# Scaling attention probabilities on GpSimd before they are turned, without a turned block of reciprocal sums, and three output products at the head of each cycle

## The chip, the cores and the metric

The kernel runs on one core of a Trainium2 chip. The metric is the device time of one execution in microseconds. The unchanged kernel took 2381.67 us, the median of three runs (2380.95 to 2384.39).

## The reference

The program is one inference step of a two-layer encoder trunk over a prompt of 2048 tokens and 8 samples of 16 tokens. Layer 0 mixes tokens by softmax attention in a band of chunks, layer 1 by a gated recurrence; each layer has a cross-attention into 256 memory tokens, a gate and an output projection. The change lies in the attention of layer 0 over the prompt:

```python
s = jnp.einsum('bcqhd,bckhd->bchqk', qc, kb).astype(F32) * (HD_A ** -0.5)
s = s + rel_bias_lookup(table, dist)
s = jnp.where(valid[None, :, None, None, :], s, NEG)
p = jax.nn.softmax(s, axis=-1).astype(v.dtype)
o = jnp.einsum('bchqk,bckhd->bcqhd', p, vb)
...
y = jnp.concatenate([mix_o, cross_attn(xq, mk, mv)], axis=-1) * jax.nn.silu(gate)
return x + y @ w
```

The softmax divides each query's exponentials by their sum. Everything is float32.

## The kernel before

The function `prompt_band` does the attention, the gating and the output projection of layer 0. A *tile* T is 128 tokens: T = 0 holds the samples, T = 1 to 16 the prompt. A tile has eight *pairs* p of heads, six of band attention (p < 6) and two of cross-attention (p = 6, 7). A *unit* is u = 8T + p. A band unit of tile T looks at n = min(T, 5) tiles of 128 keys, a cross unit at n = 2. Prompt units are worked two at a time; a *cycle* is the two units u and u+1, so a tile has four cycles, p = 0, 2, 4, 6, and the prompt has 64.

The order on each engine is written out by hand; engines meet only at semaphores. One unit and head h goes through these steps:

- TensorE `scores` (L2321, for cross units L2308) makes query by key products in PSUM.
- VectorE `low_min` adds the bias, negates and finds the row minimum (L2524, for cross units L2512).
- ScalarE `exp` (L2676) writes the exponentials into the SBUF tile `se` and their sum into `tot`.
- TensorE `turn` (L2352) turns `se` by 128x128 transposes into PSUM, n of them.
- ScalarE `low` (L2683) and VectorE `high` (L2541) copy the turned blocks to `pt` in SBUF.
- TensorE `values` (L2408) multiplies them with the values into the PSUM bank `OB`, which is transposed: its partitions are head columns, its columns are tokens.

The exponentials are not divided. Instead VectorE takes the reciprocals of both heads' sums in one instruction (`inverse`, L2530), GpSimd spreads them to a 128x128 block `rb` (`spread`, L2221), TensorE turns that block as one more transpose behind the second head's (L2356), VectorE copies it with the second head's high part, and GpSimd multiplies the gate by it (L2230). VectorE's `gate` (L2578) then multiplies `OB` by that gate for four units at once.

TensorE's order within a cycle is `turn(u,0)`, three products, `turn(u,1)`, three products, `turn(u+1,0)`, three products, `turn(u+1,1)`, three products, then `scores(u+2)`, `scores(u+3)`, `values(u)`, `values(u+1)`. The products (L2453) are those of the output projection of the tile before, 48 a tile. In the first cycle of tiles 2 to 16 the group that would stand between `turn(u+1,0)` and `turn(u+1,1)` stands ahead of `turn(u,0)` instead. VectorE's order is four copies with a reciprocal behind the first, one sum or low part (L2591 or L2583), four `low_min` of the next two units, a reciprocal, and after p = 2 and p = 6 the `gate`. GpSimd also issues the store of each finished tile (L2214), once a tile. In tile 1 VectorE also makes low parts of the weights (L2570).

Of the kernel before, what the change touches and what calls it, by code (L numbers as in the profile page):

```python
# [16 lines left out]
ALU = mybir.AluOpType  # L17
# [3 lines left out]
P = 128  # L21
# [1905 lines left out]
def prompt_band(nc, l, sem, sb_in, sb_far_in, ps_in, v, early, opening):  # L1927
# [8 lines left out]
    FIRST = (6, 0, 7, 1, 2, 3, 4, 5)  # L1936
    s_sc, s_min, s_exp, s_rs, s_tp, s_eva, s_evd, s_pv, s_gr = (
        sem(f"pb_{n}") for n in ("sc", "min", "exp", "rs", "tp", "eva", "evd", "pv", "gr"))
    s_tv, s_va, s_vd, s_y, s_yh, s_yl, s_op, s_xadd, s_bias, s_rb = (
        sem(f"pb_{n}") for n in ("tv", "va", "vd", "y", "yh", "yl", "op", "xadd", "bias", "rb"))  # L1940
    s_kt, s_kea, s_ked, s_tk, s_tka, s_tkd, s_off, s_wl, s_wh = (
        sem(f"pb_{n}") for n in ("kt", "kea", "ked", "tk", "tka", "tkd", "off", "wl", "wh"))
    s_ldk, s_ldx = ([sem(f"pb_{n}{i}") for i in range(2)] for n in ("ldk", "ldx"))
# [8 lines left out]
    with ExitStack() as ctx:  # L1952
# [71 lines left out]
        def tiles_of(T, p):  # L2024
            if T == 0:
                return 4 if p < XP else 3
            return min(T, RING) if p < MG else NMEM // P
# [17 lines left out]
        def gate_loads(job):  # L2045
            return 16 * (job // 2 + 1) + (16 if job % 2 == 0 else 0)
# [32 lines left out]
        with nc.Block() as block:  # L2079
# [130 lines left out]
            @block.gpsimd  # L2210
            def _(pool):
                def store(job):
                    pool.wait_ge(s_xadd, 2 * job + 2)
                    pool.dma_start(v["x_mid"][tile_of(job)], xt[job % 2][:]).then_inc(s_stx[job % 2], 16)  # L2214

                def spread(u):

                    at = 2 * (u % 2)
                    pool.wait_ge(s_rs, u + 1)
                    wait(pool, s_tp, 2 * u - 2)  # L2220
                    nc.gpsimd.tensor_copy(rb[u % 2][:].rearrange("p (h n) -> p h n", n=HD),  # L2221
                                          rs[:, at:at + 2].unsqueeze(2).to_broadcast([P, 2, HD])).then_inc(s_rb, 1)
                for u in range(U_ALL):
                    T, p = step(u)
                    n = tiles_of(T, p)
                    spread(u)
                    if p == 0:
                        pool.wait_ge(s_ldg[T % 2], gate_loads(T))
                    pool.wait_ge(s_evd, 2 * u + 2)
                    nc.gpsimd.tensor_tensor(gt[T % 2][:, p], gt[T % 2][:, p], pt[u % 2][1][:, n * P:(n + 1) * P], ALU.mult  # L2230
                                            ).then_inc(s_gr, 1)
                    if T == 0 and p == 5:
                        pool.wait_ge(s_pb1, 16)
                        pool.wait_ge(s_gr, u + 1)
                        nc.gpsimd.memset(bias[0:64, :, BAND - CHUNK:], BIG).then_inc(s_bias, 1)
                        pool.wait_ge(s_bias, 1)
                    if T == 1 and p == MG:
                        pool.wait_ge(s_pb2, 16)
                        pool.wait_ge(s_gr, u + 1)
                        nc.gpsimd.memset(bias[64:P, :, 0:CHUNK], BIG).then_inc(s_bias, 1)  # L2240
                        pool.wait_ge(s_bias, 2)
                    if T and p == PAIRS - 1:
                        store(T - 1)
                for t in range(early.COUNT):
                    early.root(nc, pool, t)

            @block.tensor
            def _(pe):
# [79 lines left out]
                def turn(u, h):  # L2328

                    T, p = step(u)  # L2330
                    n = tiles_of(T, p)
                    low = low_of(n)
                    done = 2 * u + h
                    to = turned_to(u, h)
                    pe.wait_ge(s_exp, done + 1)
                    if T == 0:
                        wait(pe, s_eva, done)
                        wait(pe, s_evd, done)
                    elif u % 2 == 0:
                        pe.wait_ge(s_exp if is_cross(T, p) else s_min, 2 * u + 3)  # L2340
                    elif h == 0 and u % 2:
                        pe.wait_ge(s_eva, 2 * u - 1)
                        pe.wait_ge(s_evd, 2 * u - 1)
                    if u == 0 and h == 0:
                        pe.wait_ge(s_tka, 1)
                        pe.wait_ge(s_tkd, 1)
                    if T == 0 and p == MG + 1 and h == 0:
                        pe.wait_ge(s_va, 2)
                        pe.wait_ge(s_vd, 2)
                    for i in range(n):  # L2350
                        at = i * P if i < low else 512 + (i - low) * P
                        ins = nc.tensor.transpose(to[:, at:at + P], se[u % 2][h][:, i * P:(i + 1) * P], ident[:])  # L2352
                    if h:
                        pe.wait_ge(s_rb, u + 1)
                        at = 512 + (n - low) * P
                        ins = nc.tensor.transpose(to[:, at:at + P], rb[u % 2][:], ident[:])  # L2356
                    ins.then_inc(s_tp, 1)
# [121 lines left out]
                scores(PAIRS + 1)  # L2479
                for u in range(PAIRS, U_ALL, 2):  # L2480
                    T, p = step(u)
                    lead = 3 if p == 0 and T > 1 else 0
                    project(T - 1, 6 * p, 6 * p + lead)
                    turn(u, 0)
                    project(T - 1, 6 * p + lead, 6 * p + 3 + lead)
                    turn(u, 1)
                    project(T - 1, 6 * p + 3 + lead, 6 * p + 6 + lead)
                    turn(u + 1, 0)
                    project(T - 1, 6 * p + 6 + lead, 6 * p + 9)
                    if p == MG and T < NT:  # L2490
                        turn_values(T + 1)
                    turn(u + 1, 1)
                    project(T - 1, 6 * p + 9, 6 * p + 12)
                    if u + 2 < U_ALL:
                        scores(u + 2)
                        scores(u + 3)
                    values(u)
                    values(u + 1)
# [6 lines left out]
            def _(dve):  # L2505
# [21 lines left out]
                def inverse(u):  # L2527
                    at = 2 * (u % 2)
                    dve.wait_ge(s_exp, 2 * u + 2)
                    nc.vector.reciprocal(rs[:, at:at + 2], tot[:, at:at + 2]).then_inc(s_rs, 1)  # L2530

                def high(u, h):
                    T, p = step(u)
                    n = tiles_of(T, p)
                    low = low_of(n)
                    dve.wait_ge(s_tp, 2 * u + h + 1)
                    if h:
                        wait(dve, s_gr, u - 1)
                    width = (n - low + h) * P
                    if width:  # L2540
                        ins = nc.vector.tensor_copy(pt[u % 2][h][:, low * P:low * P + width], turned_to(u, h)[:, 512:512 + width])  # L2541
                    else:
                        ins = nc.vector.memset(pt[u % 2][h][:, BAND:BAND + 1], 0.0)
                    ins.then_inc(s_evd, 1)
# [76 lines left out]
                        values_high(1)  # L2621
                low_min(PAIRS + 1, 0)
                low_min(PAIRS + 1, 1)
                inverse(PAIRS)
                for u in range(PAIRS, U_ALL, 2):
                    T, p = step(u)
                    high(u, 0)
                    inverse(u + 1)
                    high(u, 1)
                    if u == PAIRS:  # L2630
                        weights_low(5)
                    high(u + 1, 0)
                    if p == MG and T < NT:
                        values_high(T + 1)
                    if u == PAIRS:
                        weights_low(6)
                    high(u + 1, 1)
                    if p % 4 == 0:
                        low_part(T - 1 if p == 0 else T, 1 - p // 4)
                    else:  # L2640
                        add(T - 1, p // 4)
                    if u + 2 < U_ALL:
                        for v in (u + 2, u + 3):
                            low_min(v, 0)
                            low_min(v, 1)
                        inverse(u + 2)
                    if u == PAIRS:
                        weights_low(7)
                    if p % 4 == 2:
                        dve.wait_ge(s_pv, u + 2)  # L2650
                        dve.wait_ge(s_gr, u + 2)
                        gate(T, p // 4)
                low_part(NT, 1)
                for i in range(4):
# [12 lines left out]
            def _(act):  # L2667
                def exp(u, h):
                    T, p = step(u)
                    at = 2 * (u % 2) + h  # L2670
                    act.wait_ge(s_min, 2 * u + h + 1)
                    if u >= 2:
                        act.wait_ge(s_rs, u - 1)
                    n = tiles_of(T, p) * P
                    src = scores_at(u, h, u % 2, NMEM // P) if is_cross(T, p) else se[u % 2][h][:, 0:n]
# [24 lines left out]

                def keys_out_low(n, dst):
                    act.wait_ge(s_tk, n + 1)
                    if n:
                        act.wait_ge(s_gr, U_ALL)
                    nc.scalar.copy(dst[:, 0:384], TP[:, 0:384]).then_inc(s_tka, 1)

                def weights_high(i):
# [784 lines left out]
```

## Time and profile before

| | us |
|---|---|
| median of three runs | 2381.67 |
| span of the profiled execution | 2376.1 |
| busy: TensorE matmul, VectorE, ScalarE, GpSimd | 2312.2, 1819.5, 1413.5, 381.0 |
| prompt tiles of the stage that changes | about 700 to 1260 |

The profile is of one execution. It gives its span from the first to the last instruction and no other time of its own; the median of the runs is 5.6 us above that span. The table of busy times covers the whole program, so it tells little about this stage, which is about a quarter of it. Rows of the stage itself stand below.

### The profile page before, as it was taken

The page shows a single profiled execution, that of the slowest core. Times are in us where ns is not written, and L with a number is a line of the kernel's source. Part 1 is how long each engine was busy: PE and PEld are TensorE (multiplying, and loading weights), DVE is VectorE, ACT ScalarE, POOL GpSimd, SP SyncE. Part 2 cuts the span into 40 slices and gives each one's busy share as a digit, 9 for nine tenths or more (in the row PEclk, how much of TensorE's full clock was granted, in tenths as well). Part 3 has the DMA queues.
Part 4 walks back from the last instruction along what each step waited for, and adds up shares of the span by engine and source line. Part 5 has one row for each costly group of instructions (what it writes and reads, how often), then busy time and mean ns, then how long its engine had stood idle before and what let it go on. Part 6 is the DMA issues. An engine that isn't in the chain of part 4 may idle for free. (4 is left out here: it accounts for less than half of the span.)

```text
span 2376.1 us, 61711 instructions
## 1 busy us (share of the span) xinstructions
PE 2312.2 (97%) x23787; PEld 2094.7 (88%) x23787; DVE 1819.5 (77%) x3555; ACT 1413.5 (59%) x3281; POOL 381.0 (16%) x585
## 2 busy tenths in 40 slices
PE   7999999999989999999999999999999989999998
PEld 4999999999967888888887999999999978888886
DVE  7889788887666656666666998797888777888885
ACT  4564666755565555555554564776757566666664
POOL 2332000000022221211112332000000112112111
PEclk9999999999999999999999999999999999999999
DMA  6886887769894222222226897886879793444442
GB/s 227 298 299 219 301 281 231 247 220 332 232 307 121 83 66 89 90 69 83 73 81 232 272 303 242 256 275 214 266 248 312 230 269 117 129 131 122 137 135 70
DMA packets 396664, 469.64 MB, mean 198 GB/s; under 512 B 39860, under 2 KB 248556, under 8 KB 396376
## 3 DMA queue, kind: packets, MB, share of 16 engines
q1 hardware_dynamic: 379832, 406.02, 54.4%
q0 software_dynamic: 14704, 54.92, 6.6%
q10 hardware_dynamic: 1840, 4.75, 0.7%
q8 instruction: 193, 3.16, 0.5%
q14 instruction: 95, 0.78, 0.1%
HBM read 318.77 MB, written 151.56 MB: 198 GB/s over the span
## 5 line engine op out<-in xcount | busy, mean ns | idle before, releaser
L1468 PE MATMUL pj_acc<-x_lo,pj_wh 128*128 128x256 f32 (+1 forms) x3080 | 780.9, 284 | 0.0
L1468 PE MATMUL pj_acc<-x_hi,pj_wh 128*128 128x256 f32 (+1 forms) x3080 | 780.8, 284 | 0.0
L1468 PEld LDWEIGHTS pj_acc<-x_hi,pj_wh 128*128 128x128 f32 x3080 | 578.4, 188 | 0.0
L1468 PEld LDWEIGHTS pj_acc<-x_lo,pj_wh 128*128 128x128 f32 x3080 | 578.4, 188 | 0.0
L509 ACT ACTIVATE pj_wh<-pj_wt 128x512 fp32r<-128x512 f32 x676 | 420.3, 634 | 255.9 <-DMA pj_wt<-tsum 175.1
L516 DVE SCALAR_TENSOR_TENSOR pj_wl<-pj_wt,pj_wh 128x512 fp32r<-128x512 f32 x676 | 467.0, 708 | 87.0 <-ACT pj_wh L509 79.3
L1464 PE MATMUL pj_acc<-x_hi,pj_wl 128*128 128x256 f32 (+1 forms) x3080 | 509.4, 287 | 13.8 <-DVE pj_wl L516 11.9
L1464 PEld LDWEIGHTS pj_acc<-x_hi,pj_wl 128*128 128x128 f32 x3080 | 425.3, 188 | 22.1 <-DVE pj_wl L516 19.5
L1307 DVE TENSOR_TENSOR pj_out<-pj_out,pj_acc 128x512 f32<-128x512 f32 (+1 forms) x448 | 320.8, 716 | 103.3 <-PE pj_acc L1468 69.7
L2541 DVE COPY pb_pt<-pb_SCTP 128x256 f32<-128x256 f32 (+2 forms) x266 | 115.8, 435 | 147.5 <-PE pb_SCTP L2352 74.3
L2676 ACT ACTIVATE pb_se<-pb_se,pb_mn 128x640 f32<-128x640 f32 (+4 forms) x208 | 154.6, 745 | 114.6 <-DVE pb_mn L2524 114.3
L2683 ACT COPY pb_pt<-pb_SCTP 128x384 f32<-128x384 f32 (+2 forms) x272 | 106.3, 391 | 123.7 <-PE pb_SCTP L2356 62.9
L2524 DVE CUSTOM_DVE_ANT_0 pb_se<-pb_SCTP,pb_bias 128x640 f32<-128x640 f32 (+4 forms) x204 | 137.6, 727 | 44.0 <-PE pb_SCTP L2321 38.8
L2352 PE MATMUL pb_SCTP<-ident,pb_se 128*128 128x128 f32 x1020 | 156.9, 276 | 3.9 <-ACT pb_se L2676 2.6
L2352 PEld LDWEIGHTS pb_SCTP<-ident,pb_se 128*128 128x128 f32 x1020 | 121.5, 140 | 38.5 <-issue 9.2
L1204 ACT COPY pj_out<-pj_acc 128x512 f32<-128x512 f32 (+1 forms) x112 | 68.5, 611 | 115.5 <-PE pj_acc L1468 107.2
L1207 ACT COPY pj_out<-pj_acc 128x256 f32<-128x256 f32 (+1 forms) x224 | 85.4, 381 | 73.5 <-PE pj_acc L1468 69.7
L2453 PE MATMUL pb_OP<-pb_woh,pb_yh 128*128 128x512 f32 x264 | 127.1, 481 | 0.0
L2230 POOL TENSOR_TENSOR pb_gate<-pb_gate,pb_pt 128x128 f32<-128x128 f32 x136 | 74.9, 551 | 259.6 <-DVE pb_pt L2541 259.6
L3043 PE MATMUL hg_OP<-woh,hg_yh 128*128 128x512 f32 x264 | 115.5, 438 | 0.0
L478 POOL TENSOR_TENSOR pj_wt<-pj_wraw 128x512 f32<-128x512 f32 x56 | 89.1, 1594 | 120.4 <-PE pj_acc L1464 86.5
L2321 PEld LDWEIGHTS pb_SCTP<-pb_k,pb_q 64*128 64x128 f32 x1152 | 86.0, 187 | 23.9 <-issue 11.6
(371 smaller groups left out, 3992.1 us busy)
## 6 DMA issues: line engine op xcount, KB each, us to landing
pj_wt<-tsum SPq DMA_DIRECT2D x546, 256.0 KB, 3.8
proj<-pj_out SPq DMA_DIRECT2D x112, 512.0 KB, 4.2
tsum<-pj_wt SPq DMA_DIRECT2D x140, 256.0 KB, 3.2
pj_wraw<-in_w_in_dram POOLq DMA_DIRECT2D x24, 1024.0 KB, 6.6
tsum<-pj_wraw SPq DMA_DIRECT2D x56, 256.0 KB, 4.2
hg_x<-x_mid SPq DMA_DIRECT2D x17, 512.0 KB, 3.7
pb_gate<-proj SPq DMA_DIRECT2D x16, 512.0 KB, 5.1
pb_x<-in_x_prompt_dram SPq DMA_DIRECT2D x16, 512.0 KB, 3.8
```

The lines of the kernel that those rows point to most:

```text
L509: nc.scalar.mul(self.hi[j][:], self.source(step), scale_of(column(step // TERMS), self.l)).then_inc(self.s_hi, 1)
L516: nc.vector.scalar_tensor_tensor(out=self.lo[j][:], in0=self.source(step), scalar=scale_of(column(step // TERMS), self.l), in1=self.hi[j][ ...
L1307: nc.vector.tensor_tensor(to, to, what, op).then_inc(s_cb, 1)
L1464: ins = nc.tensor.matmul(BANK[j][:, 0:n], w.lo[j][:, k], x.of(x.hi, p, j)[:, k], start=(k == 0), stop=False)
L1468: ins = nc.tensor.matmul(BANK[j][:, 0:n], w.hi[j][:, k], x.of(y, p, j)[:, k], start=False, stop=(k == 3 and i == 1))
L2352: ins = nc.tensor.transpose(to[:, at:at + P], se[u % 2][h][:, i * P:(i + 1) * P], ident[:])
L2453: ins = nc.tensor.matmul(sum_of(job, half), (yl if part == 2 else yh)[job % 2][:, k], (wol if part == 1 else woh)[:, group_of(job, k), cs] ...
L2524: nc.vector.tensor_tensor_reduce(se[u % 2][h][:, 0:n * P], scores_at(u, h, 0, n), add, 1.0, 3e38, ALU.add, ALU.min, mn[:, at:at + 1]).then ...
L2541: ins = nc.vector.tensor_copy(pt[u % 2][h][:, low * P:low * P + width], turned_to(u, h)[:, 512:512 + width])
L2676: nc.scalar.activation(se[u % 2][h][:, 0:n], src, ACT.Exp, bias=mn[:, at:at + 1], scale=-1.0, accum_out=tot[:, at:at + 1]).then_inc(s_exp, 1)
L2683: nc.scalar.copy(pt[u % 2][h][:, 0:at], turned_to(u, h)[:, 0:at]).then_inc(s_eva, 1)
L3043: nc.tensor.matmul(to[:], yh[:, s], woh[:, g, cs], start=(s == 0), stop=False)
```

## The change

For prompt tiles GpSimd multiplies the exponentials in `se` by the reciprocal of their sum, in place, once per unit and head, before TensorE turns them (`normalise`). `spread`, the turned block and the multiplication of the gate remain for tile 0 only. TensorE waits for `s_nm`, which GpSimd raises, where it waited for `s_exp`. VectorE takes reciprocals one head at a time (`inverse_of`). The copies of a prompt tile's second head lose 128 columns. In all cycles but the very first, one group of three products stands at the head and `turn(u+1,1)` follows `turn(u+1,0)` directly.

```diff
-                for u in range(U_ALL):
+                def normalise(u, h):
+
                     T, p = step(u)
-                    n = tiles_of(T, p)
+                    at, n = 2 * (u % 2) + h, tiles_of(T, p) * P
+                    pool.wait_ge(s_rs, 2 * u - PAIRS + h + 1)
+                    nc.gpsimd.tensor_scalar(se[u % 2][h][:, 0:n], se[u % 2][h][:, 0:n], rs[:, at:at + 1], None, ALU.mult
+                                            ).then_inc(s_nm, 1)
+                for u in range(PAIRS):
...
+                for u in range(PAIRS, U_ALL):
+                    T, p = step(u)
+                    for h in range(2):
+                        normalise(u, h)
...
-                    if T and p == PAIRS - 1:
+                    if p == PAIRS - 1:
                         store(T - 1)
...
-                    pe.wait_ge(s_exp, done + 1)
+                    if T:
+                        pe.wait_ge(s_nm, done - 2 * PAIRS + 1)
+                    else:
+                        pe.wait_ge(s_exp, done + 1)
...
-                    if h:
+                    if h and T == 0:
                         pe.wait_ge(s_rb, u + 1)
...
-                    lead = 3 if p == 0 and T > 1 else 0
+                    lead = 3 if p or T > 1 else 0
...
+                def inverse_of(u, h):
+                    at = 2 * (u % 2) + h
+                    dve.wait_ge(s_exp, 2 * u + h + 1)
+                    nc.vector.reciprocal(rs[:, at:at + 1], tot[:, at:at + 1]).then_inc(s_rs, 1)
...
-                    width = (n - low + h) * P
+                    width = (n - low + (h if T == 0 else 0)) * P
...
                     T, p = step(u)
+                    inverse_of(u + 1, 0)
                     high(u, 0)
-                    inverse(u + 1)
+                    inverse_of(u + 1, 1)
                     high(u, 1)
...
-                        for v in (u + 2, u + 3):
-                            low_min(v, 0)
-                            low_min(v, 1)
-                        inverse(u + 2)
+                        low_min(u + 2, 0)
+                        low_min(u + 2, 1)
+                        low_min(u + 3, 0)
+                        inverse_of(u + 2, 0)
+                        low_min(u + 3, 1)
+                        inverse_of(u + 2, 1)
...
                         dve.wait_ge(s_pv, u + 2)
-                        dve.wait_ge(s_gr, u + 2)
+                        dve.wait_ge(s_ldg[T % 2], gate_loads(T))
                         gate(T, p // 4)
```

The places below are in a tile with n = 5. `pb_se` is the tile of exponentials, `pb_rb` the spread reciprocals, `pb_OP` the bank of the output projection; waits stand in brackets. TensorE before, in a cycle p = 2, from its first transpose on:

```order
L2352 MATMUL pb_SCTP<-ident,pb_se 128x128 [waits pb_min,pb_exp]
L2352 MATMUL pb_SCTP<-ident,pb_se 128x128 x4
L2453 MATMUL pb_OP<-pb_woh,pb_yh 128x512 [waits pb_yh]
L2453 MATMUL pb_OP<-pb_wol,pb_yh 128x512
L2453 MATMUL pb_OP<-pb_woh,pb_yl 128x512 [waits pb_yl]
L2352 MATMUL pb_SCTP<-ident,pb_se 128x128 [waits pb_min,pb_exp]
L2352 MATMUL pb_SCTP<-ident,pb_se 128x128 x4
L2356 MATMUL pb_SCTP<-ident,pb_rb 128x128 [waits pb_rb]
```

TensorE now, at the same place:

```order
L2466 MATMUL pb_OP<-pb_woh,pb_yh 128x512 [waits pb_yh]
L2466 MATMUL pb_OP<-pb_wol,pb_yh 128x512
L2466 MATMUL pb_OP<-pb_woh,pb_yl 128x512 [waits pb_yl]
L2365 MATMUL pb_SCTP<-ident,pb_se 128x128 [waits pb_min,pb_nm]
L2365 MATMUL pb_SCTP<-ident,pb_se 128x128 x4
L2466 MATMUL pb_OP<-pb_woh,pb_yh 128x512
L2466 MATMUL pb_OP<-pb_wol,pb_yh 128x512
L2466 MATMUL pb_OP<-pb_woh,pb_yl 128x512
L2365 MATMUL pb_SCTP<-ident,pb_se 128x128 [waits pb_min,pb_nm]
L2365 MATMUL pb_SCTP<-ident,pb_se 128x128 x4
```

The group of products moved ahead of the first turning, the `pb_rb` transpose is gone, and the wait is for `pb_nm`. VectorE before, at the head of a tile, from the third `low_min` to the first copy of turned blocks:

```order
L2524 ISA pb_se10,pb_mn<-pb_SCTP,pb_bias 128x640
L2524 ISA pb_mn 128x1
L2524 ISA pb_se11,pb_mn<-pb_SCTP,pb_bias 128x640
L2524 ISA pb_mn 128x1
L2530 RECIPROCAL pb_rs<-pb_tot 128x2
L2578 TENSOR_TENSOR pb_y1<-pb_OB,pb_gate1 128x512
L2541 COPY pb_pt00<-pb_SCTP 128x256
```

VectorE now, at the same place:

```order
L2537 ISA pb_se10,pb_mn<-pb_SCTP,pb_bias 128x640
L2537 ISA pb_mn 128x1
L2548 RECIPROCAL pb_rs<-pb_tot 128x1
L2537 ISA pb_se11,pb_mn<-pb_SCTP,pb_bias 128x640
L2537 ISA pb_mn 128x1
L2548 RECIPROCAL pb_rs<-pb_tot 128x1
L2596 TENSOR_TENSOR pb_y0<-pb_OB,pb_gate0 128x512
L2548 RECIPROCAL pb_rs<-pb_tot 128x1
L2559 COPY pb_pt00<-pb_SCTP 128x256
```

The reciprocal of the first unit's first head moved from behind the fourth `low_min` to behind the third, and the other three heads have one each behind it.

## Rows read from the trace of the kernel before

**Rows 1.** Busy time by stretch: the prompt tiles, then one tile (T = 9).
```profile
700.00:1260.00 560.00, 555.54 (x5162) 459.76 (x5162) 347.61 (x942) 297.35 (x813) 116.30 (x272) 1.00 0.31 95
1000.45:1037.56 37.11, 37.11 (x360) 31.40 (x359) 23.00 (x59) 19.84 (x51) 7.08 (x17) 1.00 0.27 79
```
**Rows 2.** Timeline of TensorE, first cycle of that tile: start, us, what.
```profile
1002.83 1.09 PE L2408 MATMUL pb_OB<-pb_pt,mem_v 128*64 128x128 f32 x16
1003.86 0.50 PE L2453 MATMUL pb_OP<-pb_woh,pb_yh 128*128 128x512 f32 x1
...
1004.66 0.71 PE L2352 MATMUL pb_SCTP<-ident,pb_se 128*128 128x128 f32 x5
1005.13 0.48 PE L2453 MATMUL pb_OP<-pb_woh,pb_yh 128*128 128x512 f32 x1
...
1005.91 0.71 PE L2352 MATMUL pb_SCTP<-ident,pb_se 128*128 128x128 f32 x5
1006.46 0.27 PE L2356 MATMUL pb_SCTP<-ident,pb_rb 128*128 128x128 f32 x1
1006.49 0.49 PE L2453 MATMUL pb_OP<-pb_woh,pb_yh 128*128 128x512 f32 x1
...
1007.28 1.25 PE L2352 MATMUL pb_SCTP<-ident,pb_se 128*128 128x128 f32 x10
...
1008.40 0.48 PE L2453 MATMUL pb_OP<-pb_woh,pb_yh 128*128 128x512 f32 x1
...
1009.28 2.46 PE L2321 MATMUL pb_SCTP<-pb_k,pb_q 64*128 64x256 f32 x28
```
**Rows 3.** Timeline of TensorE, cycles p = 2 and p = 6 of that tile.
```profile
1014.00 0.77 PE L2352 MATMUL pb_SCTP<-ident,pb_se 128*128 128x128 f32 x5
...
1019.37 0.49 PE L2321 MATMUL pb_SCTP<-pb_k,pb_q 64*128 64x256 f32 x2
...
1032.86 0.44 PE L2352 MATMUL pb_SCTP<-ident,pb_se 128*128 128x128 f32 x2
...
1037.56 0.49 PE L2321 MATMUL pb_SCTP<-pb_k,pb_q 64*128 64x256 f32 x2
```
**Rows 4.** Timeline of VectorE, ScalarE and GpSimd, first cycle; last row: cycle p = 2.
```profile
1002.06 0.82 DVE L2524 CUSTOM_DVE_ANT_0 pb_se<-pb_SCTP,pb_bias 128x640 f32<-128x640 f32 x1 [0.81 <-PE pb_SCTP L2321]
...
1003.67 0.19 ACT L2676 ACTIVATION_READ_ACCUMULATOR pb_se<-pb_se,pb_mn 128x1 f32 x1
...
1004.29 0.08 DVE L2524 DVE_READ_ACCUMULATOR2_ANT pb_mn<- 128x1 f32 x1
...
1005.04 0.16 DVE L2530 RECIPROCAL pb_rs<-pb_tot 128x2 f32<-128x2 f32 x1
...
1005.27 0.28 POOL L2221 COPY pb_rb<-pb_rs 128x128 f32<-128x128 f32 x1 [3.14 <-DVE pb_rs L2530]
...
1010.89 0.82 DVE L2524 CUSTOM_DVE_ANT_0 pb_se<-pb_SCTP,pb_bias 128x640 f32<-128x640 f32 x1 [1.05 <-PE pb_SCTP L2321]
```
**Rows 5.** GpSimd's groups by shape, whole program: busy us, mean ns.
```profile
L1622 POOL COPY sm_offs<-sm_par 128x512 f32<-128x512 f32 x1 | 0.6, 612 | 0.1
L1602 POOL MEMSET hg_masks<- 128x768 f32 x1 | 0.7, 742 | 0.1
L1629 POOL TENSOR_TENSOR wol<-wor,woh 128x1024 fp32r<-128x1024 f32 x2 | 5.1, 2566 | 20.4 <-ACT woh L1900 20.4
```
**Rows 6.** Timeline of TensorE, GpSimd and VectorE in tile 1.
```profile
708.49 0.33 PE L2352 MATMUL pb_SCTP<-ident,pb_se 128*128 128x128 f32 x1 [0.33 <-ACT pb_se L2676]
...
710.34 0.33 PE L2356 MATMUL pb_SCTP<-ident,pb_rb 128*128 128x128 f32 x1 [0.69 <-POOL pb_rb L2221]
710.42 0.48 PE L2453 MATMUL pb_OP<-pb_woh,pb_yh 128*128 128x512 f32 x1
...
709.08 1.21 POOL L2221 COPY pb_rb<-pb_rs 128x128 f32<-128x128 f32 x1 [1.61 <-DVE pb_rs L2530]
...
708.93 1.21 DVE L2570 TENSOR_TENSOR pb_wol<-pb_wraw,pb_woh 128x1024 fp32r<-128x1024 f32 x1
```

More of the change, by code:

```diff
@@ L1938, in prompt_band @@
         sem(f"pb_{n}") for n in ("sc", "min", "exp", "rs", "tp", "eva", "evd", "pv", "gr"))
-    s_tv, s_va, s_vd, s_y, s_yh, s_yl, s_op, s_xadd, s_bias, s_rb = (
-        sem(f"pb_{n}") for n in ("tv", "va", "vd", "y", "yh", "yl", "op", "xadd", "bias", "rb"))
+    s_tv, s_va, s_vd, s_y, s_yh, s_yl, s_op, s_xadd, s_bias, s_rb, s_nm = (
+        sem(f"pb_{n}") for n in ("tv", "va", "vd", "y", "yh", "yl", "op", "xadd", "bias", "rb", "nm"))
     s_kt, s_kea, s_ked, s_tk, s_tka, s_tkd, s_off, s_wl, s_wh = (
@@ L2222, in spread @@
                                           rs[:, at:at + 2].unsqueeze(2).to_broadcast([P, 2, HD])).then_inc(s_rb, 1)
-                for u in range(U_ALL):
+                def normalise(u, h):
                     T, p = step(u)
-                    n = tiles_of(T, p)
+                    at, n = 2 * (u % 2) + h, tiles_of(T, p) * P
[3 more added lines that the diff above has]
+                for u in range(PAIRS):
+                    n = tiles_of(0, u)
                     spread(u)
-                    if p == 0:
-                        pool.wait_ge(s_ldg[T % 2], gate_loads(T))
+                    if u == 0:
+                        pool.wait_ge(s_ldg[0], gate_loads(0))
                     pool.wait_ge(s_evd, 2 * u + 2)
-                    nc.gpsimd.tensor_tensor(gt[T % 2][:, p], gt[T % 2][:, p], pt[u % 2][1][:, n * P:(n + 1) * P], ALU.mult
+                    nc.gpsimd.tensor_tensor(gt[0][:, u], gt[0][:, u], pt[u % 2][1][:, n * P:(n + 1) * P], ALU.mult
                                             ).then_inc(s_gr, 1)
-                    if T == 0 and p == 5:
+                    if u == 5:
                         pool.wait_ge(s_pb1, 16)
@@ L2236, in _ @@
                         pool.wait_ge(s_bias, 1)
+                for u in range(PAIRS, U_ALL):
+                    T, p = step(u)
+                    for h in range(2):
+                        normalise(u, h)
                     if T == 1 and p == MG:
                         pool.wait_ge(s_pb2, 16)
-                        pool.wait_ge(s_gr, u + 1)
+                        pool.wait_ge(s_nm, 2 * (u - PAIRS) + 2)
                         nc.gpsimd.memset(bias[64:P, :, 0:CHUNK], BIG).then_inc(s_bias, 1)
                         pool.wait_ge(s_bias, 2)
-                    if T and p == PAIRS - 1:
+                    if p == PAIRS - 1:
                         store(T - 1)
@@ L2536, in high @@
                     dve.wait_ge(s_tp, 2 * u + h + 1)
-                    if h:
+                    if h and u < PAIRS + 2:
                         wait(dve, s_gr, u - 1)
-                    width = (n - low + h) * P
+                    width = (n - low + (h if T == 0 else 0)) * P
                     if width:
@@ L2623, in _ @@
                 low_min(PAIRS + 1, 1)
-                inverse(PAIRS)
+                inverse_of(PAIRS, 0)
+                inverse_of(PAIRS, 1)
                 for u in range(PAIRS, U_ALL, 2):
                     T, p = step(u)
+                    inverse_of(u + 1, 0)
                     high(u, 0)
-                    inverse(u + 1)
+                    inverse_of(u + 1, 1)
                     high(u, 1)
@@ L2671, in exp @@
                     act.wait_ge(s_min, 2 * u + h + 1)
-                    if u >= 2:
+                    if 2 <= u < PAIRS + 2:
                         act.wait_ge(s_rs, u - 1)
@@ L2702, in keys_out_low @@
                     act.wait_ge(s_tk, n + 1)
-                    if n:
-                        act.wait_ge(s_gr, U_ALL)
                     nc.scalar.copy(dst[:, 0:384], TP[:, 0:384]).then_inc(s_tka, 1)
```

## The prediction

> **What bounds the kernel now.** I read the busy time by stretch first. In the prompt tiles TensorE is busy 555.5 of 560 us and in the tile I take as pattern 37.11 of 37.11, while VectorE has 23.0, ScalarE 19.8 and GpSimd 7.1 [rows 1]. So in a full tile only what TensorE does, or is made to wait for, counts; VectorE and GpSimd have room. The modelled ends of matmuls hide short waits, so I then read TensorE's timeline and go by distances between starts. From tile 5 on, where n = 5, the tiles are alike.
>
> In the first cycle of the tile the values of the cross units take 1.03 us, three products 0.80 us (1003.86 to 1004.66), five transposes 0.47, three products 0.78, five transposes and the block of sums 0.58 (1005.91 to 1006.49), three products 0.79, eleven transposes 1.12, and the last three products with the turn to the scores 0.88 [rows 2]. The cycle p = 2 takes 5.37 us from its first transpose to the next scores, the cycle p = 6 4.70 [rows 3]. Last I read the three engines that make the probabilities: when the first reciprocal could be there, and when GpSimd could start on it [rows 4].
>
> **What is removed.** A cycle loses two transposes of the sums. One costs 0.11 us of TensorE: 0.58 for six against 0.47 for five [rows 2]. In 64 cycles that is up to 14.1 us; no other engine covers it, because TensorE is the one that is full. The spread, the gate multiplication and 128 columns of a copy also go, but they lie on engines with idle time and I cost them at nothing. GpSimd's idle stretch before its copy is 3.14 us [rows 4], VectorE is busy for 23.0 of 37.1 [rows 1].
>
> **What is moved.** In cycles p = 2, 4, 6 a group of products goes to the head and the last two turnings become neighbours. The new cycle p = 2 can be put together from the pieces of the first cycle, which already has this order: 0.80 + 0.47 + 0.78 + 0.47 + 0.78 + 1.01 (eleven transposes less one) + 0.88 = 5.19, against 5.37 [rows 2, 3]. So 0.18 of the 0.22 arrive, and I take the same for p = 4 and p = 6. The first cycle, whose order stays, gets 0.22. A full tile without a new wait is shorter by 0.22 + 3 x 0.18 = 0.76 us. The copies between the two neighbouring turnings and the next scores have the 0.88 us of products as cover, as they have in the first cycle now; if the cover were gone, a copy of half a microsecond would be exposed. No DMA changes its place: the store at a tile's end waits for the same sum and stands ahead of the first scaling as it stood ahead of the first spread.
>
> **What is added.** TensorE now turns only after: third `low_min` done, reciprocal, GpSimd's scaling of 128x640 in place. In the first cycle of the tile the exponentials are ready at 1003.67 + 0.19 = 1003.86, but VectorE is in the third `low_min` until its read-out at 1004.29. The reciprocal then stands at 1004.29 (as now at 1005.04 behind the fourth) and takes 0.16. GpSimd starts 0.07 behind a reciprocal (1005.20 to 1005.27), so at 1004.52 [rows 4].
>
> How long the scaling takes no row shows. GpSimd's copy takes 0.28 us for 128 columns [rows 4] and 0.61 for 512 [rows 5]; the line through both gives 0.72 at 640. From below the fill bounds it: 0.74 for 768, so 0.62 for 640. From above the operation with two tiles as input: 2.57 for 1024, so 1.60. I take 0.75, next to the copies, because the scaling too reads one tile and writes one. The first result is then there at 1005.27. TensorE starts some 0.05 us after a GpSimd release (709.08 + 1.21 = 710.29 to 710.34), and its next product follows 0.08 behind the transpose instead of 0.03, as weights were not loaded ahead [rows 6]. The first turning now starts at 1004.66; it would be late by 0.61 + 0.06 + 0.06 = 0.73 us. Queued behind that transpose is all of TensorE, so the wait is added whole. In the old form the same head could be turned before its reciprocal existed.
>
> The Trainium skill, GPSIMD Engine Reference, "3.1 Elementwise — side-by-side cycle accounting", puts the best case of an elementwise loop at about 1.8 cycles of 1.2 GHz per element and two inputs at about 2.6. The rows above show 0.86 ns per column for a copy, about one cycle. By the page's 1.8 the scaling would be an estimated 0.96 us, the stall of a full tile 0.94, and the sum below about 2.5 us less favourable.
>
> Elsewhere the scaling hides. In cycle p = 2 the turning has 0.80 us of products ahead of it and comes no sooner than 1014.00 + 0.80 = 1014.80. The first `low_min` of its units starts at 1010.89, and GpSimd at 1010.89 + 2.46 = 1013.35 by the distance of the first cycle (1002.06 to 1004.52); the scaling ends at 1014.10 [rows 2, 3, 4]. The fourth turning comes at 1017.85, the fourth scaling could end at 1013.35 + 4 x 0.75 = 1016.35. This breaks from 1.11 us a scaling. The third head's reciprocal is queued behind the gate after p = 2 and 6, but even then over a microsecond before its turning. The reciprocals are one more instruction per unit of 0.16 us on VectorE, which has room.
>
> **The sum.** Tiles 5 to 16: 12 x (0.73 - 0.76) = -0.4 us. Tiles 2 to 4 have shorter `low_min` and scalings; each can have a stall between 0 and 0.73, and I take 0.6 for the three together, and 0.2 gained in tile 2 where the head products fill small waits: 0.6 - 3 x 0.76 - 0.2 = -1.9. Tile 1, with one block per head, has waits now: 0.33 us for an exponential at 708.49, and at 710.34 for the spread, which was held up beside a VectorE operation (1.21 instead of 0.28) [rows 6]. The scaling of that head is held up by the same operation, but a group of products of 0.78 us now lies ahead of the wait: -0.8. The next cycle has its wait for an exponential filled, -0.4, the other two get 0.2 each. Tile 1: -1.6. Together -3.9 us. The profiled execution spans 2376.1, 5.6 below the median of the runs, so a difference in it is taken over: 2381.7 - 3.9 = 2377.8. What a measurement can tell from no change is about 0.2%, 4.8 us; the forecast lies inside.
>
> **Rivals.** *Slower: GpSimd can't follow.* The four scalings of a cycle run back to back on one engine, and from 1.11 us each the fourth decides everywhere, not only the first at a tile's head. At 1.2 us the first cycle's fourth result is there at 1004.52 + 4.8 + 0.06 = 1009.38 where its turning starts at 1007.83 now (1007.28 and five transposes): 1.55 late. In p = 2 and 4 it is 1018.21 against 1017.85: 0.36 each. A full tile is 1.55 + 0.72 - 0.76 = 1.5 us longer, twelve 18 us; with the small tiles +15, 2397. At the upper end, 1.60, the same sum gives some +74, 2455. For it speaks that GpSimd needs 2.57 us for 1024 columns with two inputs, against it the copy's line [rows 5]. Chance 0.19.
>
> *Faster: no wait at a tile's head.* If the reciprocal is not behind the third `low_min` in effect, or the lost time is made up on TensorE later in the tile, all of it arrives: 15 x 0.76 + 0.2 + 1.6 = 13.2, 2368.5. Against it stands that the pattern tile shows no idle TensorE into which a delay could be absorbed [rows 1]. Chance 0.12.
>
> *The change removes a wait rather than work.* Then only tile 1 would move, by 1.6 us, to 2380. It needs the transposes of the sums to be free, against which 0.58 and 0.47 stand [rows 2]. Chance 0.05.
>
> **How the numbers follow.** The forecast's case has 0.64. Its own range, with scalings of 0.62 to 1.0 us (twelve stalls of 0.60 to 1.0) and 1.5 us of noise, is 2374.5 to 2382.5. It falls beyond -4.8 us in about a third of its cases, 0.21, so faster is 0.21 + 0.12 = 0.33. Slower is the second case, mostly, and a remainder of the first: 0.20. The rest, 0.47, is no change. For 8 in 10 I go down to 2371, toward the full gain, and up to 2394, just short of the price of 1.2 us a scaling.
>
> **What would show it.** Right: about 5.2 us instead of 5.37 from the head products to the next scores in cycles p = 2 and 4, 128 transposes fewer, a wait of TensorE for GpSimd's scaling about 0.6 us long once a tile from tile 5 on and at no other place, scalings of 0.7 to 0.8 us, a tile of about 37.1 us as before. Wrong: scalings above 1.1 us and waits before the fourth turning in every band cycle; or first cycles as short as 8.6 us; or copies to `pt` that hold up the scores.

## The result and the profile after

The changed kernel takes 2512.8 us, the median of four runs (2512.2 to 2519.2), against 2383.0 before on the same chip: a ratio of 1.055, 95% interval 1.0537 to 1.0565. The prediction was 2377.8 with a range of 2371 to 2394. The change was forecast to gain 3.9 us and lost 130, or 5.5%; the time lies 135 us above the forecast, far outside the range. The rival "GpSimd can't follow" is what happened, beyond the upper end that the prediction gave it for the duration of a scaling.

The busy time by stretch of the changed kernel (columns as in rows 1): all prompt tiles, then the tile that answers to the one of rows 1.

```profile
700.00:1390.00 690.00, 583.86 (x5020) 439.22 (x5019) 339.72 (x1065) 303.48 (x810) 386.69 (x270) 0.98 0.26 78
1065.53:1112.55 47.02, 38.97 (x352) 29.92 (x351) 22.61 (x67) 20.29 (x51) 26.67 (x17) 1.00 0.21 63
```

The tile takes 47.02 us where it took 37.11 [rows 1]. (Counted by the scores of the cross units it is the tenth prompt tile, not the ninth; the tiles from 5 on are alike, 37.05 us on average before and 47.03 now, so nothing hangs on it.) VectorE and ScalarE do what they did; GpSimd went from 7.1 to 26.7 us of work in one tile, and TensorE, which was busy throughout, now has 8 us without any. Twelve such tiles are 119 us of the 130.

GpSimd's groups by shape in that stretch (columns as in rows 5):

```profile
L2228 POOL TENSOR_SCALAR pb_se<-pb_se,pb_rs 128x640 f32<-128x640 f32 x144 | 269.1, 1884 | 162.6 <-DVE pb_rs L2548 162.6
L2228 POOL TENSOR_SCALAR pb_se<-pb_se,pb_rs 128x256 f32<-128x256 f32 x76 | 69.3, 925 | 65.9 <-DVE pb_rs L2548 65.9
L2228 POOL TENSOR_SCALAR pb_se<-pb_se,pb_rs 128x512 f32<-128x512 f32 x12 | 18.6, 1564 | 11.5 <-DVE pb_rs L2548 11.5
L2228 POOL TENSOR_SCALAR pb_se<-pb_se,pb_rs 128x384 f32<-128x384 f32 x12 | 14.7, 1244 | 9.4 <-DVE pb_rs L2548 9.4
```

A scaling of 640 columns takes 1.88 us. The steps from width to width are 0.32 us per 128 columns, 2.5 ns a column, with about 0.28 us on top. The prediction had taken 0.75.

TensorE's timeline in the first cycle of that tile; it answers to rows 2. A bracket says how long the engine was idle and who released it.

```profile
1068.94 0.49 PE L2466 MATMUL pb_OP<-pb_woh,pb_yh 128*128 128x512 f32 x1
...
1071.59 0.76 PE L2365 MATMUL pb_SCTP<-ident,pb_se 128*128 128x128 f32 x5 [1.69 <-POOL pb_se L2228]
1072.11 0.49 PE L2466 MATMUL pb_OP<-pb_woh,pb_yh 128*128 128x512 f32 x1
...
1073.46 0.77 PE L2365 MATMUL pb_SCTP<-ident,pb_se 128*128 128x128 f32 x5 [0.39 <-POOL pb_se L2228]
...
1075.32 0.77 PE L2365 MATMUL pb_SCTP<-ident,pb_se 128*128 128x128 f32 x5 [0.39 <-POOL pb_se L2228]
1077.18 0.76 PE L2365 MATMUL pb_SCTP<-ident,pb_se 128*128 128x128 f32 x5 [1.10 <-POOL pb_se L2228]
...
1078.58 0.49 PE L2331 MATMUL pb_SCTP<-pb_k,pb_q 64*128 64x256 f32 x2
```

GpSimd in the same cycle, one row for four instructions in a row:

```profile
1069.65 7.48 POOL L2228 TENSOR_SCALAR pb_se<-pb_se,pb_rs 128x640 f32<-128x640 f32 x4 [2.43 <-DVE pb_rs L2548]
```

The reader should see two things. The four turnings stand 1.87, 1.86 and 1.86 us apart, which is GpSimd's duration and nothing of TensorE's. And the chain's start is where the prediction put it: GpSimd begins 4.12 us behind the first scores (1065.53), against 4.07 foreseen (1004.52 less 1000.45). Only the length of its four links is new.

### The profile page after: what moved, and what is told of

Read it like the earlier page. It is cut to its first block and busy times, and to the rows that moved or that the text cites. A ratio compares the mean times of both kernels' runs of the same rounds, so it can differ in the third digit from the quotient of the medians.

```text
span 2517.4 us, 61058 instructions
## 1 busy us (share of the span) xinstructions
PE 2349.0 (93%) x23659; PEld 2079.7 (83%) x23659; DVE 1817.9 (72%) x3683; ACT 1423.0 (57%) x3281; POOL 653.2 (26%) x585
## 5 line engine op out<-in xcount | busy, mean ns | idle before, releaser
L2228 POOL TENSOR_SCALAR pb_se<-pb_se,pb_rs 128x640 f32<-128x640 f32 (+4 forms) x256 | 379.6, 1497 | 261.3 <-DVE pb_rs L2548 261.3
L2559 DVE COPY pb_pt<-pb_SCTP 128x256 f32<-128x256 f32 (+1 forms) x260 | 98.0, 377 | 285.0 <-PE pb_SCTP L2365 284.2
L2365 PE MATMUL pb_SCTP<-ident,pb_se 128*128 128x128 f32 x1020 | 170.4, 288 | 106.9 <-POOL pb_se L2228 106.0
L2365 PEld LDWEIGHTS pb_SCTP<-ident,pb_se 128*128 128x128 f32 x1020 | 115.0, 143 | 186.4 <-POOL pb_se L2228 176.1
L2331 PE MATMUL pb_SCTP<-pb_k,pb_q 64*128 64x128 f32 (+1 forms) x1152 | 105.4, 329 | 1.6 <-issue 1.6
```

What stands on the lines that cost most here:

```text
L2228: nc.gpsimd.tensor_scalar(se[u % 2][h][:, 0:n], se[u % 2][h][:, 0:n], rs[:, at:at + 1], None, ALU.mult).then_inc(s_nm, 1)
```

## The experiments

Three theories were set against each other: A, the scaling's own duration is the whole loss; B, the new place of the products and turnings costs a good part; C, GpSimd and VectorE hold each other up.

**No scaling at all.**

```diff
-                    for h in range(2):
-                        normalise(u, h)
...
-                    if T:
-                        pe.wait_ge(s_nm, done - 2 * PAIRS + 1)
-                    else:
-                        pe.wait_ge(s_exp, done + 1)
+                    pe.wait_ge(s_exp, done + 1)
```

> The changed kernel without the scaling: GpSimd leaves the probabilities of the prompt tiles unscaled, TensorE waits for the exponentials again; new order, single reciprocals and shorter copies stay. Before 2383, changed 2513. Theory A (the scaling's own duration, 1.88 us for 128x640, four in a row on GpSimd, is the whole loss): full saving of the removed transposes, 13 us, so about 2370; cycles p = 2 at 9.9 us, waits of TensorE for GpSimd gone. Theory B (the new order of products and turnings costs a good part): well above 2400. Theory C (GpSimd and VectorE hold each other up at their shared port): as A here.

2366.0 us against 2383.3, ratio 0.9927 (0.9908 to 0.9946). That excludes B. It gives what the change is worth without the new link: 17 us (13 to 22 by the interval), where the prediction's second rival had 13.2. Between the first scores of the tiles, a full tile takes 36.31 us on average against 37.05, 0.75 less, where 0.76 were foreseen. What goes beyond stands in the small tiles: tiles 2 to 4 gain 4.2 us together (89.5 to 85.3) where 2.5 were foreseen, tile 1 some 4 where 1.6 were. All 130 us of loss and these 17 come in with the scaling.

**The scaling cut to 128 columns.**

```diff
+                    n = min(n, P)
                     nc.gpsimd.tensor_scalar(se[u % 2][h][:, 0:n], se[u % 2][h][:, 0:n], rs[:, at:at + 1], None, ALU.mult
```

> The changed kernel with each scaling cut to the first 128 of its columns, all waits kept; the other columns stay unscaled. Theory A: a scaling takes 0.60 to 0.67 us, near the 0.75 the prediction took, so the time lands where the prediction put it, 2379 (a wait of 0.6 to 0.7 us once a tile, no other). Theory B: above 2400 still. Theory C (held up beside VectorE): the 128-column scalings would be long too, 0.9 us and more, and the time 2385 to 2400.

2376.3 against 2383.3, ratio 0.9971 (0.9959 to 0.9983). The same 256 scalings at the same places with the same waits now make the kernel faster:

```profile
L2229 POOL TENSOR_SCALAR pb_se<-pb_se,pb_rs 128x128 f32<-128x128 f32 x256 | 153.5, 606 | 340.5 <-DVE pb_rs L2549 339.2
```

They take 0.606 us, beside the same VectorE work. In the full tiles the shortest and the longest differ by 5 ns (602 and 607). In the changed kernel the mean of the 144 instructions of 640 columns is 1884 ns and the longest of the full tiles takes 1889. Nothing is held up in the steady tiles, so C is out. (In tile 1 of the changed kernel, 128 columns take 0.666 us on average; there something may hold them up.) With links of this length the kernel is 7 us faster, where 3.9 were predicted.

**A copy in its place.**

```diff
-                    nc.gpsimd.tensor_scalar(se[u % 2][h][:, 0:n], se[u % 2][h][:, 0:n], rs[:, at:at + 1], None, ALU.mult
-                                            ).then_inc(s_nm, 1)
+                    nc.gpsimd.tensor_copy(se[u % 2][h][:, 0:n], se[u % 2][h][:, 0:n]).then_inc(s_nm, 1)
```

> The changed kernel with GpSimd's scaling replaced by a copy of the same 128x640 tile onto itself; the probabilities stay unscaled. Theory A, in the form that the scaling's kind of instruction is slow: the copy takes about 0.72 us, as the line through the two copies of the trace says, and the time is 2379. If what makes it slow is the place (beside ScalarE, VectorE and TensorE on the same tile) and not the operation, the copy takes 1.5 to 1.9 us too and the time is 2460 to 2513.

2375.3 against 2383.3, ratio 0.9966 (0.9951 to 0.9981).

```profile
L2228 POOL COPY pb_se<-pb_se 128x640 f32<-128x640 f32 x144 | 101.9, 722 | 199.5 <-DVE pb_rs L2547 195.8
L2228 POOL COPY pb_se<-pb_se 128x256 f32<-128x256 f32 x76 | 30.3, 400 | 102.4 <-DVE pb_rs L2547 100.2
```

The line through two copies, 0.72 us at 640 columns, was right, for copies. TensorE at the head of the tile:

```profile
997.84 2.46 PE L2330 MATMUL pb_SCTP<-pb_k,pb_q 64*128 64x256 f32 x28
...
1002.69 0.77 PE L2364 MATMUL pb_SCTP<-ident,pb_se 128*128 128x128 f32 x5 [0.47 <-POOL pb_se L2228]
```

The first turning stands 4.85 us behind the first scores, 4.21 before (1004.66 less 1000.45 in rows 2): 0.64 late, where the prediction had 0.73, and from tile 4 on that is the only wait for GpSimd that the trace shows, once a tile. A full tile takes 37.01 us on average against 37.05 before (0.05 less before rounding), where the prediction has 0.03 less. So near the duration that the prediction used, its working for a full tile comes out. The whole is less exact than it looks: 2375.3 lies 2.5 us from the forecast of 2377.8, but against the unchanged kernel of the same runs the gain is 8.0 us (4.5 to 11.7), twice the 3.9 foreseen. Of the rest tiles 2 to 4 give 3.7 us instead of 1.9. The width, the place and the tile are the same as in the changed kernel; the operation makes 0.72 or 1.88.

**The order alone, on the unchanged kernel.**

```diff
-                    lead = 3 if p == 0 and T > 1 else 0
+                    lead = 3 if p or T > 1 else 0
```

> The unchanged kernel with only the group of three products moved to the head of every cycle but the first. Theory A: 48 cycles lose or gain under 0.05 us each, so 2381 to 2386 against 2383. Theory B: 2400 or more.

2384.5 against 2383.3, ratio 1.0002 (0.9989 to 1.0015): no difference, so the move alone costs nothing that can be measured. The tile takes 37.15 us where it took 37.11:

```profile
967.25:1004.40 37.15, 37.15 (x347) 30.89 (x347) 22.95 (x59) 19.95 (x51) 7.08 (x17) 1.00 0.27 79
```

**The scaling cut to 384 columns.**

```diff
+                    n = min(n, 3 * P)
                     nc.gpsimd.tensor_scalar(se[u % 2][h][:, 0:n], se[u % 2][h][:, 0:n], rs[:, at:at + 1], None, ALU.mult
```

> The changed kernel with each scaling cut to at most 384 columns, all waits kept; the rest stays unscaled. Its duration is then that of the changed kernel's 384-column form, 1.24 us. Theory A with the prediction's chain (fourth result at 4 scalings behind the first reciprocal): first cycle 1.73 us late, p = 2 and 4 0.54 each, so a full tile 2.05 longer than before, twelve of them 25, small tiles -3: 2383 + 21 = 2404. Rival: the loss goes straight with the summed GpSimd time (1.24/1.88 of 130 + 13, less 13), which gives 2464.

2417.6 against 2381.7, ratio 1.0145 (1.0131 to 1.0159). Neither 2404 nor 2464.

```profile
L2229 POOL TENSOR_SCALAR pb_se<-pb_se,pb_rs 128x384 f32<-128x384 f32 x168 | 206.1, 1241 | 183.6 <-DVE pb_rs L2549 183.6
L2229 POOL TENSOR_SCALAR pb_se<-pb_se,pb_rs 128x256 f32<-128x256 f32 x76 | 69.2, 923 | 66.1 <-DVE pb_rs L2549 66.0
```

For full tiles the chain's working holds: 2.05 us more a tile was expected, 2.3 measured (cycles of 10.48, 10.46, 10.47 and 7.92 us between first scores, 39.33 against 37.05 before). It failed in the small tiles, for which the expectation took over the prediction's gain of some 3 us. In tiles 2 and 3 rows have 256 and 384 columns, so the cut takes nothing away; TensorE has fewer matmuls to hide four scalings behind, and a band cycle of tile 3 takes 9.02 us against 7.47. Tiles 2 to 4 together lost 9.3 us (89.5 to 98.8). The prediction's step "each can have a stall between 0 and 0.73" was therefore no bound either, once the scaling is slow.

**A constant instead of the pointer.**

```diff
-                    nc.gpsimd.tensor_scalar(se[u % 2][h][:, 0:n], se[u % 2][h][:, 0:n], rs[:, at:at + 1], None, ALU.mult
+                    nc.gpsimd.tensor_scalar(se[u % 2][h][:, 0:n], se[u % 2][h][:, 0:n], 1.0, None, ALU.mult
```

> The changed kernel with the same scaling instruction, but a constant 1.0 in place of the pointer to the reciprocal per partition (the probabilities stay unscaled). If the pointer operand makes the instruction slow: 0.7 to 0.8 us each and 2379. If the kind of instruction does: 1.88 us and 2513.

2494.6 against 2381.7, ratio 1.0468 (1.0454 to 1.0482).

```profile
L2228 POOL TENSOR_SCALAR pb_se<-pb_se 128x640 f32<-128x640 f32 x144 | 256.9, 1806 | 162.3 <-DVE pb_rs L2548 162.3
```

1.81 us: the pointer costs 0.08 us an instruction and nothing per column (at 256 columns it is 0.848 against 0.925). The kind of instruction is slow, as a multiplication in float32; no other operation was tried. The 0.08 in each of twelve scalings accounts for most of the 18 us that this run is faster than the changed kernel.

**The same multiplication with two tiles as input.**

```diff
-                    nc.gpsimd.tensor_scalar(se[u % 2][h][:, 0:n], se[u % 2][h][:, 0:n], rs[:, at:at + 1], None, ALU.mult
+                    nc.gpsimd.tensor_tensor(se[u % 2][h][:, 0:n], se[u % 2][h][:, 0:n], rs[:, at:at + 1].to_broadcast([P, n]), ALU.mult
```

> The changed kernel with the scaling written as a multiplication of two tiles, the second the reciprocal broadcast along the row (same result). By the rows of two-input operations, 0.46 us at 128 columns and some 2.1 ns more a column, 1.53 us at 640; the chain then gives 2.87 late in the first cycle, 1.68 in p = 2 and 4, a full tile +5.5, 2383 + 65 = 2448. If the second input's broadcast costs nothing: copies' rate, 0.75 us and 2379. If it costs as the pointer form: 1.88 us, 2513.

2398.9 against 2381.7, ratio 1.0068 (1.0054 to 1.0082). The expectation took the wrong duration again, 1.53 us; it is 1.25:

```profile
L2228 POOL TENSOR_TENSOR pb_se<-pb_se,pb_rs 128x640 f32<-128x640 f32 x144 | 176.0, 1251 | 162.2 <-DVE pb_rs L2548 162.2
L2228 POOL TENSOR_TENSOR pb_se<-pb_se,pb_rs 128x256 f32<-128x256 f32 x76 | 44.9, 613 | 79.9 <-DVE pb_rs L2548 79.8
```

The form that names two tiles is a third faster, 1.25 against 1.88 us; 2.5 ns a column become 1.66. Its second input is one value per partition, repeated, so this says nothing of two full tiles. With 1.25 in the chain the full tile works out as it was measured: the fourth result of the first cycle at 1004.52 + 5.0 + 0.06 = 1009.58, 1.75 behind 1007.83, in p = 2 and 4 0.56, less 0.76, so 2.1 us longer; measured 39.24 against 37.05. Twelve such tiles make 26 us where the whole kernel lost 17; tiles 2 to 4 gain 1.6, and where the other 7 went isn't shown. This one-line edit takes back 114 of the 130 us.

**The scaling on VectorE.**

```diff
-                    for h in range(2):
-                        normalise(u, h)
...
+                def scale(u, h):
+                    T, p = step(u)
+                    at, n = 2 * (u % 2) + h, tiles_of(T, p) * P
+                    dve.wait_ge(s_rs, 2 * u - PAIRS + h + 1)
+                    nc.vector.tensor_scalar(se[u % 2][h][:, 0:n], se[u % 2][h][:, 0:n], rs[:, at:at + 1], None, ALU.mult
+                                            ).then_inc(s_nm, 1)
...
                     inverse_of(u + 1, 0)
+                    scale(u + 1, 0)
                     high(u, 0)
                     inverse_of(u + 1, 1)
+                    scale(u + 1, 1)
...
                         low_min(u + 3, 0)
                         inverse_of(u + 2, 0)
+                        scale(u + 2, 0)
                         low_min(u + 3, 1)
                         inverse_of(u + 2, 1)
+                        scale(u + 2, 1)
```

> The changed kernel with the scaling on VectorE, each directly behind its reciprocal (same result; GpSimd does none for prompt tiles). VectorE's scaling instructions of this width take about 0.55 us in the trace. Theory A: the first cycle waits about 0.5 us at its head, no other cycle waits, so a full tile is 0.26 shorter than before: 2383 - 7 = 2376. Rival: VectorE, with 2.2 us more a cycle, becomes the bound in cycles p = 2 and 4: 2390 to 2410.

2382.4 against 2381.7, ratio 1.0001 (0.9988 to 1.0014): no difference, neither theory's number. Cycles p = 2 and 4 take 9.90 us, as they do with the copy, so VectorE is not the bound there. The first cycle takes 9.70. VectorE in it:

```profile
999.61 0.55 DVE L2552 TENSOR_SCALAR pb_se<-pb_se,pb_rs 128x640 f32<-128x640 f32 x1
...
1001.48 0.68 DVE L2601 TENSOR_TENSOR pb_y<-pb_OB,pb_gate 128x512 f32<-128x512 f32 x1
1002.08 0.15 DVE L2546 RECIPROCAL pb_rs<-pb_tot 128x1 f32<-128x1 f32 x1
1002.27 0.55 DVE L2552 TENSOR_SCALAR pb_se<-pb_se,pb_rs 128x640 f32<-128x640 f32 x1
1002.74 0.42 DVE L2564 COPY pb_pt<-pb_SCTP 128x256 f32<-128x256 f32 x1
```

and TensorE's third and fourth turning there, in one row:

```profile
1003.30 1.33 PE L2363 MATMUL pb_SCTP<-ident,pb_se 128*128 128x128 f32 x10 [0.21 <-DVE pb_pt L2564]
```

The first turning is 0.44 late, as expected (0.5). But the third waits as well, and by the bracket not for its scaling but for the first head's copy, which frees the PSUM it writes; that copy is queued behind the gate, a reciprocal and a scaling.

**Split between both engines, the gate moved.** The cut shows the change against the version with VectorE alone.

```diff
                         scale(u + 2, 0)
                         low_min(u + 3, 1)
                         inverse_of(u + 2, 1)
                         scale(u + 2, 1)
+                        inverse_of(u + 3, 0)
...
-                    inverse_of(u + 1, 0)
-                    scale(u + 1, 0)
                     high(u, 0)
+                    if u > PAIRS and p % 4 == 0:
+                        Tg, pg = step(u - 2)
+                        dve.wait_ge(s_pv, u)
+                        dve.wait_ge(s_ldg[Tg % 2], gate_loads(Tg))
+                        gate(Tg, pg // 4)
...
+                    if u % 2:
+                        normalise(u, 0)
```

Here `normalise` is the two-input form, with a semaphore of its own.

> The changed kernel with the scaling split (same result): VectorE scales both heads of the first unit of a cycle and the second head of the second, GpSimd the first head of the second with the two-input form (1.25 us); VectorE's gate moved behind the next unit's first copy. Theory: what kept the version with VectorE alone at 2382 is its first cycle of a tile (9.70 us: 0.44 late at the first turning, 0.4 more at the third, which stands behind the gate on VectorE). The 0.4 goes, a tile is about 37.0 us, the time 2376. Rival: VectorE's total load, not its order, made that wait, and the time stays 2380 to 2384.

2375.5 against 2380.7, ratio 0.9976 (0.9967 to 0.9986), the time that the theory gave. The first cycle falls from 9.70 to 9.41 us and the tile from 37.4 to 37.1. The edit does two things at once, though: it moves the gate and it takes one scaling in four off VectorE (29.95 to 28.68 us of work a tile), out of the same queue ahead of the copy. Which of them gave the 0.3 us isn't shown.

**And six products at the head of a tile.**

```diff
-                    lead = 3 if p or T > 1 else 0
+                    lead = 0 if u == PAIRS else 6 if p == 0 else 3
...
-                    project(T - 1, 6 * p + 9, 6 * p + 12)
+                    project(T - 1, max(6 * p + 9, 6 * p + 6 + lead), 6 * p + 12)
```

> As the split version, and in the first cycle of tiles 2 to 16 six products stand at the head and none behind the last turning (same result). Theory: the first scaling is then hidden, the first cycle falls to about 8.7 us, a tile to 36.4, the time to about 2370. Rival: the scores of the next units now wait for the copies to SBUF that the last three products covered, 0.5 to 0.9 us a tile, and the time is 2376 to 2380.

2370.0 against 2380.7, ratio 0.9957 (0.9945 to 0.9970). TensorE in the first cycle:

```profile
998.63 0.40 PE L2469 MATMUL pb_OP<-pb_woh,pb_yh 128*128 128x512 f32 x1
...
999.32 0.71 PE L2368 MATMUL pb_SCTP<-ident,pb_se 128*128 128x128 f32 x5
...
1001.89 1.31 PE L2368 MATMUL pb_SCTP<-ident,pb_se 128*128 128x128 f32 x10
1003.26 0.49 PE L2332 MATMUL pb_SCTP<-pb_k,pb_q 64*128 64x256 f32 x2
```

No bracket is left. The scores follow 1.37 us behind the third turning, where the pieces of rows 2 give about 1.1 (ten transposes 1.01, and 0.09 for the turn to the scores), so I estimate that the copies that are now uncovered cost some 0.3. The tile takes 36.54 us. This version beats the kernel before by 0.43% and the changed one by some 5.6%.

**The changed kernel with the old place of the products.**

```diff
-                    lead = 3 if p or T > 1 else 0
+                    lead = 3 if p == 0 and T > 1 else 0
```

> The changed kernel with the old place of the products (at the head only in the first cycle of tiles 2 to 16). Theory A: four scalings of 1.88 us in a row set the length of every band cycle whatever the products do, so 2513 within 0.5%. Rival: the products at the head hide part of the first scaling and their move back costs up to 0.8 us in each of 48 cycles, 2520 to 2550.

2514.5 against 2380.7 (ratio 1.0562, 1.0547 to 1.0576) where the changed kernel has 1.0551 (1.0537 to 1.0565). The cycles p = 2 are 13.02 and 13.03 us. When four scalings of 1.88 us set the length, nothing that TensorE does in another order counts.

## Why the prediction was wrong

**What bounds the kernel.** Right: full tiles were TensorE's, and VectorE had room; the split version gives it 5.7 us more a tile (28.7 against 23.0) and is faster.

**What is removed.** Right in kind, a little low: 13.2 us in sum was foreseen for the change without a wait, 17 measured in the kernel without scaling. The full tiles were right (0.75 against 0.76); the small tiles were taken too low.

**What is moved.** Right: 5.19 us was put together for the products and turnings of p = 2, so a cycle of 9.89, and the version with the copy has cycles of 9.88 to 9.92. Alone, the order changes nothing that can be measured.

**What is added: this is the step that failed.** "I take 0.75, next to the copies, because the scaling too reads one tile and writes one." It takes 1.88. The copy's price is the copy's, 0.722 us. For the kind of instruction there was no row at all, and counting the tiles it reads did not stand in for one. The upper bound of 1.60 failed as well. It came from one operation with two tiles as input, 2.57 us for 1024 columns, and the trace of the kernel before holds a slower one, outside the prompt tiles:

```profile
L478 POOL TENSOR_TENSOR pj_wt<-pj_wraw 128x512 f32<-128x512 f32 x56 | 89.1, 1594 | 120.4 <-PE pj_acc L1464 86.5 <-POOLq L721 28.8 <-DMA x_mid<-pb_x 4.1
```

In proportion to the columns its mean gives 1.99 us at 640 and its median of 1.416 gives 1.77; the prediction's own chain then makes the full tiles 132 or 100 us longer. It is no row of `tensor_scalar` either, but it would have kept the bound open to what came. What makes it slower than the row that was used isn't known.

**The chain.** Right, once the true duration is in it. The prediction's own working with 1.88: first cycle 1004.52 + 7.52 + 0.06 = 1012.10, 4.27 behind 1007.83; in p = 2 and 4 1020.93 against 1017.85, 3.08 each; less 0.76 makes 9.7 us a tile. Measured 9.9. Its limit of 1.11 us a scaling fits the runs: at 0.72 the fourth turning of the full tiles doesn't wait, at 1.25 it does; the value itself was not bracketed closer. With the tiles 5 to 16 at 119 us of 130 (9.9 each), the small tiles did not gain 3.5 but lost some 11; tiles 2 to 4 alone went from 89.5 to 102.7 us. For these the prediction had no chain, only "a stall between 0 and 0.73".

**The rate per column.** The prediction set the 1.8 cycles per element of the Trainium skill, GPSIMD Engine Reference, "3.1 Elementwise — side-by-side cycle accounting", against the rows' one cycle and kept to the rows. Counted in those cycles of 1.2 GHz, by the runs the copy needs one per column (0.84 ns from 256 to 640), the two-input form with a broadcast operand 2.0 (1.66 ns), `tensor_scalar` 3.0 (2.5 ns). The Trainium skill, GPSIMD Engine Reference, "4.1 Engine selection", calls one-input operations roughly line-rate; the copy agrees, `tensor_scalar` does not, and the measurement decides.

**The chances.** 0.19 for GpSimd falling behind and an upper end of 2394 were too little for an unknown whose two bounds, 0.62 and 1.60, already led to 2376 and 2455 by the prediction's own sum. The range was cut at 1.2 us a scaling without a row that excluded more.

## What to carry to other kernels

When a change brings a kind of instruction that the trace does not hold on that engine, don't let a single row of another kind bound it: here the copy was 2.6 times too fast and the one two-input row that was used still too fast. Work out the duration from which the chain decides, and if the unknown can plausibly pass it, let the range reach there. Several such instructions in a row on one engine multiply the error: here 1.13 us too little in one became 9.9 a tile. On GpSimd, where the widths are like these, multiply by a per-partition value with the two-input form and a broadcast operand, or put the scaling on an engine with room, and then look at what is queued behind it.

## What the runs showed that was not expected

- On GpSimd `tensor_scalar` by a pointer takes 0.28 us and 2.5 ns a column (0.606 at 128, 1.884 at 640), with a constant 0.08 us less; `tensor_tensor` with the second input broadcast 1.251 at 640; a copy onto itself 0.722; `tensor_scalar` on VectorE 0.554.
- Small tiles are more, not less, exposed to a slow link: with 1.24 us scalings the cycle p = 2 of tile 3 lost 1.5 us (7.47 to 9.01), that of a full tile 0.4 (10.07 to 10.46). Only at the head of a tile are they alike, 1.7 each.
- The change without its scaling was worth 17 us of 2383. In full tiles that is 0.09 us for each of the eight small transposes that a tile loses; in the small tiles waits go with them.
